# Loading an expert's second weights between the two halves of a later expert's first weights, for experts 15 to 28 of a streamed mixture of experts

## What is computed

```python
    for e in range(N_EXPERTS):                                   # 32
        z = jnp.einsum('bsd,df->bsf', h, w1[e]) + b1[e]          # w1[e]: 1024 x 2048
        glu = jnp.minimum(z[..., 0::2], SWIGLU_LIMIT)
        lin = jnp.clip(z[..., 1::2], -SWIGLU_LIMIT, SWIGLU_LIMIT)
        act = glu * jax.nn.sigmoid(SWIGLU_ALPHA * glu) * (lin + 1.0)
        out = out + combine[..., e:e + 1] * (jnp.einsum('bsf,fd->bsd', act, w2[e]) + b2[e])
```

## Time and profile before

| | us |
|---|---|
| median of 3 runs | 1082.29 |
| the three runs | 1081.51, 1082.29, 1082.70 |
| the profiled execution | 1082.48 |
| its span, from first to last instruction | 1080.7 |
| PE busy within the span | 1039.1 (96%) |
| DVE busy | 302.9 (28%) |
| ACT busy | 157.1 (15%) |
| POOL busy | 22.5 (2%) |

### The profile page before, as it was taken

One profiled execution on the slowest core, in us unless ns is written; L12 is line 12 of the kernel. 1 busy time (PEld: TensorE's weight loads), 2 busy tenths in 40 slices (PEclk: granted clock), 3 DMA queues, 4 the chain that ended last, 5 costly groups with the idle time before them and its releaser, 6 DMA issues.

```text
span 1080.7 us, 11540 instructions
## 1 busy us (share of the span) xinstructions
PE 1039.1 (96%) x4616; PEld 400.2 (37%) x4616; DVE 302.9 (28%) x704; ACT 157.1 (15%) x282; POOL 22.5 (2%) x29
## 2 busy tenths in 40 slices
PE   8999999999999999899998999898989899999997
PEld 7458454333333333233333333233333233333332
DVE  2455622422222222132221222221323222221231
ACT  1231333110101111101010111011101101111112
POOL 1212000000000000000000000000000000000000
PEclk9999999999999999999998999999999999999999
DMA  9886947999999999999999999999999999999995
GB/s 326 241 245 268 379 176 317 384 432 412 431 431 431 431 428 432 434 429 431 428 429 431 435 430 428 434 433 432 429 433 433 432 429 434 432 432 431 425 429 230
DMA packets 33050, 429.79 MB, mean 398 GB/s; under 512 B 4892, under 2 KB 6336, under 8 KB 16352
## 3 DMA queue, kind: packets, MB, share of 16 engines
q1 hardware_dynamic: 31104, 426.03, 93.6%
q10 hardware_dynamic: 1216, 1.70, 1.1%
q0 software_dynamic: 704, 1.71, 0.6%
HBM read 426.80 MB, written 2.62 MB: 397 GB/s over the span
## 4 chain that ended last, share of the span: by engine, by line
PE 70%; DMA 27%; DVE 1%; SPq 1%; issue 1%; ACT 0%; DVEq 0%
PE ps L1361 31%; DMA w1r<-w_mlp 22%; PE ps L1389 13%; PE ps L1430 5%; PE ps L1110 4%; PE ps L1339 3%; PE ps L1098 3%; DMA w2r<-w_mlp 2%; DMA w1r<-w_out 1%; PE ps L1157 1%; PE ps L1263 1%; PE ps L1232 1%; PE ps L1403 1%; DMA w1r<-w_in 1%; PE ps L1347 1%; PE ps L1369 1%
## 5 line engine op out<-in xcount | busy, mean ns | idle before, releaser
L1361 PE MATMUL ps<-w1r,arena 128*64 128x512 f32 x2040 | 484.9, 611 | 22.4 <-DMA w1r<-w_mlp 22.0
L1361 PEld LDWEIGHTS ps<-w1r,arena 128*64 128x64 f32 x2040 | 141.8, 139 | 285.8 <-issue 279.6
L1389 PE MATMUL ps<-w2r,arena 128*64 128x512 f32 x960 | 212.0, 593 | 7.3 <-DMA w2r<-w_mlp 7.3
L1389 PEld LDWEIGHTS ps<-w2r,arena 128*64 128x64 f32 x960 | 68.0, 137 | 147.1 <-issue 131.4
L981 DVE TENSOR_TENSOR acc<-ps,acc 128x512 f32<-128x512 f32 x56 | 36.1, 686 | 175.1 <-PE ps L1430 175.1
L973 DVE TENSOR_TENSOR arena<-arena 128x512 f32<-128x512 f32 x32 | 22.2, 692 | 163.5 <-ACT arena L593 163.4
L935 DVE TENSOR_TENSOR arena<-ps,cols 128x512 f32<-128x512 f32 x31 | 21.4, 692 | 139.3 <-PE ps L1347 139.3
L597 ACT ACTIVATE arena<-ps 128x512 f32<-128x512 f32 x31 | 18.5, 597 | 288.4 <-PE ps L1369 288.3
L1339 PE MATMUL ps<-h,arena 128*64 128x512 f32 x248 | 58.7, 592 | 0.0
L602 ACT ACTIVATE arena<-ps 64x512 f32<-64x512 f32 x29 | 17.2, 592 | 269.5 <-PE ps L1389 269.5
L1430 PE MATMUL ps<-arena 128*128 128x512 f32 x112 | 55.5, 618 | 0.0
(11 more groups left out here) (257 smaller groups left out, 579.4 us busy)
## 6 DMA issues: line engine op xcount, KB each, us to landing
w1r<-w_mlp SPq DMA_DIRECT2D x54, 4096.0 KB, 30.9
w2r<-w_mlp SPq DMA_DIRECT2D x32, 2048.0 KB, 18.7
w2r<-w_mlp SPq DMA_DIRECT2D x14, 4096.0 KB, 20.8
w1r<-w_mlp SPq DMA_DIRECT2D x17, 2048.0 KB, 10.3
w1r<-w_in SPq DMA_DIRECT2D x7, 2048.0 KB, 17.1
w1r<-w_mlp SPq DMA_DIRECT2D x12, 1024.0 KB, 8.3
w1r<-w_out SPq DMA_DIRECT2D x2, 2048.0 KB, 13.7
rel_table<-arena ACTq DMA_DIRECT2D x1, 1536.0 KB
```

The lines of the kernel that those rows point to most:

```text
L1361: ins = mm(ps[64 * c:64 * c + 64, 2 * par + n, :], hgT[:, par, k % 4, 64 * (k // 4):64 * (k // 4) + 64], cols_z, start=False, stop=(k == 7))
L1389: ins = mm(ps[at:at + 64, 4 + c, :], actT[:, k % 4, 64 * (k // 4):64 * (k // 4) + 64], w2r[:, k // 2, col:col + 512], start=(k == 0), stop ...
```

## The change

The helper between takes the way of loading w2 as a parameter, and the loop for e = 15 to 28 calls between in place of ahead, still with the whole 4 MB transfer. The three transfers of a turn are the same ones with the same waits; their order goes from w2[e], half 0, half 1 to half 0, w2[e], half 1. Nothing on the other engines is changed.

```diff
-                def between(e, x, par):
+                def between(e, x, par, load=next_w2):
                     next_half(base, x, par, 0)
-                    next_w2(base, e)
+                    load(base, e)
                     next_half(base, x, par, 1)
...
                 with sp.Fori(8, NE // 2 - 1) as m:
-                    ahead(2 * m - 1, 2 * m + 1, 1, next_w2_whole)
-                    ahead(2 * m, 2 * m + 2, 0, next_w2_whole)
+                    between(2 * m - 1, 2 * m + 1, 1, next_w2_whole)
+                    between(2 * m, 2 * m + 2, 0, next_w2_whole)
```

## The result

The changed kernel takes 1090.98 us, the median of six runs (1086.57 to 1092.23), beside 1082.49 us for the kernel before (1081.16 to 1083.38): a ratio of 1.0069, 95% interval 1.0053 to 1.0085, or 8.5 us more. A second series, on another occasion, gave 1090.03 beside 1082.37 us, 1.0070 (1.0056 to 1.0084), 7.7 us more. Forecast were 7.3 us more and 1089.6 us, in a range of 1087.3 to 1091.8; both medians lie inside it.

The account below looks back on a forecast made before the run. Transfers were taken to bound the loop and PE everything after down(28) at 1002.45 us. 5.65 us for the order plus 1.7 us for the clock, given as 7.3 us late, made 1089.6 us, range 1087.3 to 1091.8.

Parts of the forecast that it names:

- The bound and the queue: In the loop: transfers set the pace, same bytes, landings 9.7 us apart without a hole, cost 0.
- The cover for w2[28]: Queue at w2[28]'s issue: 12.5 us of transfers still in line, so the queue does not run dry.
- rival B: Seam between turns: half 0 ready a turn sooner makes transfers faster, 1080 us or less; chance 2%.
- Where w2 lands: In the loop: w2[e] lands one transfer later, half 0 one earlier; w2[28] at 1008.0 us.
- The steady state: Pair of steps: 53.53 us of PE against 58.3 of transfers; gap up to 4.7 us before odd experts' down.
- The handover: At down(28), where PE stops waiting for transfers: starts at 1008.1 instead of 1002.45 us, 5.65 us late.
- The clock: Behind the gap before down(27): low granted clock adds 1.7 us, bounds 0 and 3.4.
- The tail: PE work from 1002.45 us on: unchanged, one idle time of 0.3 us; the end moves by 7.3 us.
- A: Loop at transfer share 1.00: only bytes count, order does not matter, end stays at 1082.3 us; chance 5%.
- C: Queue in the loop: w2 issued over 12.5 us late, 21 us lost in seven pairs, 1110 us; chance 3%.

Follow-up runs that it names:

- last_pair_undone: Changed kernel with the old order taken back for experts 27 and 28, new order kept for 15 to 26; 1085.48 us beside 1082.37 for the kernel before.
- filled_short: Changed kernel plus 8 useless matmuls before the w2 wait in every odd expert's down from 15 on; 1088.44 us beside 1082.73 for the kernel before.
- changed_again: The changed kernel measured once more with no edit; 1090.03 us beside 1082.37 for the kernel before.
- last_pair_alone: Kernel before with the new order for experts 27 and 28 alone, old order for 15 to 26; 1090.84 us beside 1082.37.
- behind_28: Kernel before with, for expert 28 alone, w2 issued behind both halves of w1[30]; 1100.25 us beside 1082.73.
- only_28: Kernel before with the new order for expert 28 alone; 1090.06 us beside 1082.73.
- only_27: Kernel before with the new order for expert 27 alone; 1089.82 us beside 1082.73.
- filled_gap: Changed kernel plus 16 useless matmuls before the w2 wait in every odd expert's down from 15 on; 1100.41 us beside 1082.37 for the kernel before.

## Why the prediction was right, point by point

**The bound and the queue.** Transfer share 1.00 and 432 GB/s as foreseen, landings 9.7 us apart. The cover for w2[28] was 1000.3 - 989.6 = 10.7 us and not 12.5: the slow down(27) and the time from its end to the issue were missing from it. It cost nothing, as the forecast had it. Two readings in the prediction's rival B were loose, without weight for the result: half 0 of w1[e + 2] is issued some 9 us sooner in the new order (with the shift of the landings taken off), in the middle of the same step, and not a turn sooner; and the slices over the turns of e = 5 to 10 show 428 to 434 GB/s, not 431 to 432.

**Where w2 lands.** One transfer behind its old place, to 0.1 us, once the 1.9 us of this execution are taken off.

**The steady state.** The forecast gap of some 3 us once in two steps, before the down of an odd expert, is there as 3.03 to 3.14 us in the last five pairs of the first profile, and the waits for first weights are gone. The first gap, where the new order begins, was forecast at some 9 us:

```profile
631.24 9.30 PE L1389 MATMUL ps<-w2r,arena 128*64 128x512 f32 x32 [9.70 <-DMA w2r<-w_mlp]
```

It costs nothing that shows at the end: last_pair_undone has a first gap of 10 us and is 3.1 us slower in all (interval 1.4 to 3.9 us), of which PE's place at its last late w2 accounts for 2.4.

**The handover.** 5.65 us for the order: filled_short measures 5.7, and its down(28) is 5.69 late. This is the term that carries the result, and undoing two of fourteen turns took most of it away.

**The clock.** Taken at 1.7 us, between 0 and 3.4; the profiles of the changed kernel show 1.5 and 1.7 us, the medians up to 2.8. That the point came out so well is in part luck: half of a stretch was a choice between two rows, and it rests on the last gap being some 3 us. In changed_again the gaps before the downs of odd experts were 2.02, 4.69 and 2.27 us before they settled at 3.03 to 3.06; the down behind 2.02 took 7.09 us and the one behind 4.69 took 9.56. With gaps of 10 and 15 us before the handover it was 2.2 (last_pair_alone) and 2.6 us (behind_28). With the 1.7 us the forecast of 7.3 us stands 0.4 and 1.2 us under the two series. The term may be short by that; the difference is within the intervals of both, and what of it is clock and what is the spread of the runs is open.

**The tail.** Taken to hold one idle time of 0.3 us that moves along. It did, and in behind_28 the tail took up nothing of 17.5 us.

**The rivals.** A (the order does not matter, 1082.3) fell with the change itself, and with it the reading that only the most-contended engine counts. The Trainium skill, Perfetto Trace Analysis, section Identifying Performance Opportunities, says only that improving a kernel generally involves improving that engine; the "alone" was the prediction's. Here the transfers were that engine in the loop, at share 1.00 and 432 GB/s in both kernels, and yet the end moved by 8 us, since PE had the lead behind the loop. B (faster) had no trace: the rate is the same. C (the queue runs dry) did not happen in the change; the kernel that goes back to the old order in the middle shows the beginning of it, 1.5 us. The Trainium skill, DMA: Bandwidth & Descriptors, section Rules for kernel authors, advises to issue a transfer early and wait for it late. In this full queue that gained nothing: half 0 of w1[30] was issued at 969.6 and not 977.1, and what it gained was w2[28]'s place. Whether it pays in a queue with room no run here shows.

## What to carry to other kernels

In a full queue like this one, a transfer that moves ahead in line makes another land later by a whole transfer, here 9.7 us. Ask which landing the consumer needs last, and at which point the consumer stops waiting for transfers and leads. Ahead of that point the order cost only the lateness that it left there (3 us for twelve turns), and from there the delay went to the end undiminished: two turns out of fourteen carried the whole loss, and one nearly all of it. The gap that the transfers leave before a matmul can also cost clock, here 1.5 to 1.7 us behind 3 us, and the last such gap stands on the path.

## What the runs showed of the hardware that I had not expected

The same gap goes with either level of the clock. The trace of the kernel before has a granted clock of 0.97 from 640 to 1003 us, with slow stretches behind gaps of 2.28 us. In only_28, whose loop is in the old order up to expert 27, the same gaps of 2.28 us went with a clock of 1.00 in that stretch. First the kernel before, then only_28:

```profile
640.00:1003.00 363.00, 344.30 (x1516) 117.25 (x1517) 85.62 (x177) 40.22 (x68) 0.00 (x0) 0.97 1.00 432
```

```profile
640.00:1003.00 363.00, 335.86 (x1520) 114.98 (x1518) 88.14 (x182) 40.21 (x68) 0.00 (x0) 1.00 1.00 432
```

Both happen even within one execution: in last_pair_alone the 16 matmuls behind such a gap took 3.65 us five times and 5.35 us the sixth time, one pair of steps later and still ahead of its first changed transfer:

```profile
862.55 3.65 PE L1363 MATMUL ps<-w1r,arena 128*64 128x512 f32 x16 [2.28 <-DMA w1r<-w_mlp]
...
920.83 5.35 PE L1363 MATMUL ps<-w1r,arena 128*64 128x512 f32 x16 [2.28 <-DMA w1r<-w_mlp]
```

So the length of such a gap does not settle what it costs, and which side an execution falls on is not set by the order of the transfers. Behind each of the four gaps of 3.0 us and more before down(27) (3.06, 3.14, 10.25 and 10.32 us) the down took 8.56 us or more in place of 7.04.

A transfer issued about 1 us before the line is empty comes too late to be seamless: in last_pair_undone, issued 1.1 us before, it landed 11.2 us behind the one before it and not 9.7, and w2[28] of only_27, issued 0.95 us before, also 11.2 us behind. With 1.6 us, in filled_gap, it was 10.6. Where the line was full, landings were 9.7 us apart, with single ones of up to 10.5.
